# Sixteen modulation turns of the second layer placed elsewhere: six in the key and query tiles, four in the dilated attention, four in the mix, two in the up projection

## The reference, cut to what matters

```
def first_block(...):
    c_act = jax.nn.silu(c)
    for l in range(DEPTH):
        ada = (c_act @ w_ada[l] + b_ada[l])[:, None, :]
        sh1, sc1, g1, sh2, sc2, g2 = jnp.split(ada, 6, axis=-1)
        u = h * (1.0 + sc1) + sh1
        y = mixer(u, ...)
        h = layer_norm(DN_ALPHA * h + g1 * y, ...)
        u = h * (1.0 + sc2) + sh2
        y = swiglu(u, w1[l], w3[l], w2[l])
        h = layer_norm(DN_ALPHA * h + g2 * y, ...)
```

## Time and profile before

| | |
|---|---|
| median of 3 runs | 2356.89 us (2355.12 to 2361.71) |
| the profiled execution | 2354.97 us |
| its span in the trace | 2353.2 us |
| mean granted clock of PE | 0.996 |
| busy: PE / DVE / ACT / POOL | 2279.4 / 1382.9 / 503.1 / 243.5 us |

### The profile page before, as it was taken

One profiled execution on the slowest core, in us unless ns is written; L12 is line 12 of the kernel. 1 busy time (PEld: TensorE's weight loads), 2 busy tenths in 40 slices (PEclk: granted clock), 3 DMA queues, 4 the chain that ended last, 5 costly groups with the idle time before them and its releaser, 6 DMA issues.

```text
span 2353.2 us, 29622 instructions
## 1 busy us (share of the span) xinstructions
PE 2279.4 (97%) x11910; PEld 1850.9 (79%) x11910; DVE 1382.9 (59%) x2532; ACT 503.1 (21%) x1083; POOL 243.5 (10%) x165
## 2 busy tenths in 40 slices
PE   7999999999999999999999999999999999989998
PEld 5888588799768885878988655588888887667987
DVE  5764234644746433367876677675566448756455
ACT  1222220110011223201010365322200023433200
POOL 0000001331000000013310000000000001001332
PEclk9999999999999999999999999999999999999999
DMA  9863438545476343575654411433433324345442
GB/s 393 331 222 108 146 117 311 213 155 177 173 275 226 108 142 127 180 258 200 210 201 170 144 36 40 149 108 126 143 116 124 110 90 162 125 152 179 157 166 81
DMA packets 163511, 391.34 MB, mean 166 GB/s; under 512 B 6448, under 2 KB 10928, under 8 KB 160560
## 3 DMA queue, kind: packets, MB, share of 16 engines
q1 hardware_dynamic: 136736, 285.03, 34.0%
q0 software_dynamic: 24080, 93.69, 11.1%
q10 hardware_dynamic: 2560, 10.72, 1.2%
HBM read 388.37 MB, written 1.05 MB: 165 GB/s over the span
## 4 chain that ended last, share of the span: by engine, by line
PE 91%; DVE 6%; ACT 1%; issue 1%; DMA 0%; SPq 0%; DVEq 0%; ACTq 0%
PE bank L548 89%; DVE arena L2087 3%; PE bank L546 2%; DVE arena L2093 2%; ACT arena L1440 1%; DMA arena<-in_w_ada 0%; DVE arena L2090 0%; ACT arena L1443 0%; DVE junk L2093 0%; DVE arena L3039 0%; ACT L1440 0%; DVE arena L2225 0%; SPq L3201 0%; DVE arena L2156 0%; SPq L3193 0%
## 5 line engine op out<-in xcount | busy, mean ns | idle before, releaser
L548 PE MATMUL bank<-arena 128*128 128x256 f32 (+5 forms) x11422 | 2225.8, 363 | 45.8 <-DVE arena L2087 17.8
L548 PEld LDWEIGHTS bank<-arena 128*128 128x128 f32 (+2 forms) x11422 | 1794.0, 189 | 464.7 <-issue 248.8
L2087 DVE TENSOR_TENSOR arena<-arena 128x1024 f32<-128x1024 f32 (+8 forms) x535 | 446.6, 849 | 228.6 <-PE bank L548 195.6
L1440 ACT ACTIVATE arena<-arena 128x512 f32<-128x512 f32 (+5 forms) x427 | 213.6, 521 | 804.3 <-DVE arena L2087 457.9
L2093 DVE SCALAR_TENSOR_TENSOR arena<-arena 128x1028 f32<-128x1028 f32 (+6 forms) x367 | 308.9, 858 | 97.6 <-DMA arena<-in_w_ada 77.4
L2087 DVE TENSOR_TENSOR arena<-arena,bank 128x256 f32<-128x256 f32 (+2 forms) x326 | 150.1, 485 | 157.0 <-PE bank L548 147.3
L3279 POOL DMA_DIRECT2D arena<-in_w_ada x88 | 62.7, 712 | 1728.0 <-DVEq L2102 1717.4
L1443 ACT ACTIVATE arena<-bank 128x512 f32<-128x512 f32 (+1 forms) x199 | 109.0, 598 | 439.3 <-PE bank L548 414.9
L2087 DVE TENSOR_TENSOR arena<-bank,arena 128x512 f32<-128x512 f32 (+3 forms) x103 | 70.1, 690 | 206.4 <-PE bank L548 184.4
L1440 ACT ACTIVATE arena<-bank 128x256 f32<-128x256 f32 (+1 forms) x121 | 50.2, 432 | 504.9 <-PE bank L548 504.2
L2093 DVE SCALAR_TENSOR_TENSOR arena<-bank,arena 128x254 f32<-128x254 f32 (+2 forms) x184 | 78.1, 469 | 51.1 <-PE bank L546 34.1
(11 more groups left out here) (37 smaller groups left out, 221.3 us busy)
## 6 DMA issues: line engine op xcount, KB each, us to landing
arena<-in_w_ada POOLq DMA_DIRECT2D x88, 1028.0 KB, 5.6
arena<-in_w_in SPq DMA_DIRECT2D x84, 1024.0 KB, 7.2
arena<-in_w SPq DMA_DIRECT2D x56, 1024.0 KB, 5.5
arena<-in_w_mlp_in SPq DMA_DIRECT2D x32, 1024.0 KB, 7.0
arena<-in_w_mlp_out SPq DMA_DIRECT2D x32, 1024.0 KB, 7.3
arena<-in_w_gla SPq DMA_DIRECT2D x12, 1024.0 KB, 6.9
arena<-in_w_ada SPq DMA_DIRECT2D x16, 514.0 KB, 19.4
arena<-in_w_a SPq DMA_DIRECT2D x8, 1024.0 KB, 7.0
```

Of the source, the lines that this page charges most:

```text
L548: ins = nc.tensor.matmul(out, lhsT, rhs, start=start, stop=stop)
L1440: return nc.scalar.activation(out, x, f, **kw)
L2087: return V.tensor_tensor(out, x, y, op)
```

## The change

The sixteen turns n = 36 to 51 keep their order and their content and get other places: one after each of the key and query tiles n = 2, 4, 6, 8, 9, 11 (the four one-condition turns and two others), one after each of the four attention units, one after WA 0, WB 0, WB 1 and WB 2 in the mix, and one after the up panels 3 and 6. POOL's queue is changed with it: the weight sums of panels 0 to 4 stand before load 52, those of 5 to 7 before load 53, those of 8 and 9 before load 54. Layer 0 is unchanged.

```
-UP_TURNS = (1, 3, 4, 6, 7, 9)
+UP_TURNS = (3, 6)
+MINI_TURNS = (2, 4, 6, 8, 9, 11)
+FIRST_UP_JOB = 52
...
+                beside = iter([(q, [("ada", 0)]) for q in ADA_TAIL] +
+                              [(q, [("next", 0)] if l + 1 < DEPTH else [("next", 1), ("nextx", 2)]) for q in ADA_NEXT] +
+                              [(q, [("ada", 1), ("adax", 2)]) for q in ADA_LATER[:4]])
...
                 for n in range(12):
                     for h, s in minis(n):
                         dve_mini(h, s)
+                    if l == DEPTH - 1 and n in MINI_TURNS:
+                        beside_mix(1)
                 for u in range(SLOTS // 2):
...
+                    if l == DEPTH - 1:
+                        beside_mix(1)
                 for p in range(2):
...
-                        beside_mix((1, 1, 1 - l, 0)[j])
+                        beside_mix(((1, 1, 1, 0), (1, 0, 0, 0))[l][j])
...
-                        beside_mix((1, 5, 0, 3 - l)[j])
+                        beside_mix(((1, 5, 0, 3), (1, 1, 1, 0))[l][j])
...
                     if l == DEPTH - 1 and at in UP_TURNS:
-                        j = UP_TURNS.index(at)
-                        if j < 2:
-                            beside_mix(1)
-                        else:
-                            ada_turn(6 + j, [("ada", 1), ("adax", 2)])
-                        if j == len(UP_TURNS) - 1:
+                        beside_mix(1)
+                        if at == UP_TURNS[-1]:
...
-                if 48 <= n < 54:
-                    for at in range((-1, *UP_TURNS)[n - 48] + 2 if n > 48 else 0, min(UP_TURNS[n - 48] + 2, len(UP))):
+                if FIRST_UP_JOB <= n < FIRST_UP_JOB + 3:
+                    for at in ((0, 1, 2, 3, 4), (5, 6, 7), (8, 9))[n - FIRST_UP_JOB]:
                         weight_sums(1, at)
```

More of the change, by code:

```diff
@@ L2635, in _, with beside_mix @@
                 dve.wait_ge(act_done, AC.at("silu 7"))
+                beside = iter([(q, [("ada", 0)]) for q in ADA_TAIL] +
+                              [(q, [("next", 0)] if l + 1 < DEPTH else [("next", 1), ("nextx", 2)]) for q in ADA_NEXT] +
+                              [(q, [("ada", 1), ("adax", 2)]) for q in ADA_LATER[:4]])
+                def beside_mix(n):
+                    for _ in range(n):
+                        q, conds = next(beside)
+                        ada_turn(q, conds)
+                        if q == ADA_TAIL[-1]:
+                            gate("g2")
                 for n in range(12):
```

## The result

The changed kernel takes 2364.10 us, median of 20 runs (2361.71 to 2366.99); the kernel before, on the same chip, takes 2360.32 us, median of 20 (2354.95 to 2363.83). The ratio is 1.0019 with a 95% interval of 1.0012 to 1.0026, so 2.8 to 6.1 us slower. That is inside the 0.3% called "no change", on the slow side of it, and 2364.1 us lies outside the predicted range of 2352.4 to 2361 us.

What follows compares the result with a forecast made beforehand. PE bounds the kernel, busy 2279.4 of 2353.2 us. Up projection -4.63, tiles and attention 0, mix +3.32 and clock +2.1 sum to +0.8 us; on 2354.97 us, plus 1.0, that gives 2356.8 us, range 2352.4 to 2361.

Steps and rivals of the forecast that it cites:

- no change, leaning slower: Whole kernel: +0.8 us in sum; chance 0.91 of staying within 7 us, 0.06 of slower.
- The base: Whole kernel: the profiled execution's 2354.97 us, plus 1.0 us for the mean of the two lower timed runs, 2356.0 us.
- Mix: +3.32 us: Second layer's mix: the turn after WB 2 delays mix 3, so WO's wait grows from 1.51 to 4.83 us.
- rival C: Mix: POOL's sum gets in before DVE's add for mix 3, 2.7 us later, +3.5 us in all; chance 0.11.
- Up projection: -4.63 us: Second layer's up projection: waits after panels 1 and 7 go (-2.13, -2.50 us), 1.27 us after panel 3 stays.
- ceiling of 5.9 us: Second layer's up projection: PE's four waits for DVE, 5.9 us together, cap the gain at 0.25% of the time.
- PE's clock: 2.1 us: Start of WO: the 4.83 us wait makes the granted clock fall, costing 2.1 us, between 0 and 2.8.
- Tiles and attention: 0: Key and query tiles, attention: the ten turns fit DVE's gaps, tightest spare 1.5 and 1.7 us, so cost 0.
- Rival D: Key and query tiles: loads land late, turns overrun at four tiles, 7.2 us, +8.0 us in all; chance 0.04.
- E: Up projection: the removed turns did not cause the waits, which stay, +5.4 us, 2361.4 us; chance 0.02.
- Rival B: Up projection: the wait after panel 3 goes too, another -1.27 us; chance 0.10.
- Rival A: WO: the clock holds despite the 4.83 us wait, -1.3 us in all, 2354.7 us; chance 0.13.

Runs made afterwards that it cites:

- the fourth experiment: The changed kernel with the turn behind WB 2 moved behind WA 2 and POOL's sums of up panel 5 ahead of load 52: 2352.08 us, ratio 0.9968.
- the fifth experiment: The kernel before, its six up projection turns in place, with only POOL's sums of panels 3, 5, 6, 8 and 9 one load earlier: 2359.24 us, ratio 0.9991.
- the first experiment: The changed kernel with only the turn behind WB 2 moved behind WA 2: 2353.81 us, ratio 0.9975.

## Why the prediction was wrong

The sign, "no change, leaning slower", and the two mechanisms (the waits of the removed turns go; the turn behind WB 2 makes WO wait and the clock fall) were right. Three steps failed: the base that the sum was added to, the mix term of +3.32 us, which let DVE's add go ahead of POOL's sum, and, the other way, the up projection's -4.63 us. The first two are the miss.

**The base.** The sum was made against an execution of 2354.97 us with a mean granted clock of 0.996, and 1.0 us was added. This was an execution on the lucky side. Of the 35 executions of the kernel before that ran beside the first experiments, one had 0.996, and eleven had 0.991:

| mean granted clock | 0.991 | 0.992 | 0.993 | 0.994 | 0.995 | 0.996 |
|---|---|---|---|---|---|---|
| executions | 11 | 6 | 7 | 3 | 7 | 1 |
| mean time, us | 2363.6 | 2361.5 | 2359.7 | 2358.0 | 2355.8 | 2356.4 |

Of the 30 beside the last experiments six had 0.996 and ten had 0.991. About 2 us go with each 0.001. The three runs shown had a median of 2356.89 us, the twenty have 2360.32. This step is worth 2360.32 - 2356.0 = 4.3 us of the miss of 7.3, and it says nothing about the change: with 4.3 us added to both ends the same range runs to 2365.3 us and holds the 2364.1 measured.

**"Mix: +3.32 us."** The turn is worth just that, 4.83 us of wait with POOL held back. But the forecast let DVE's add go first because it would start 0.17 us before POOL's sum. The start came out as computed (0.15 us), and DVE lost all the same, 2.38 us. That was rival C, with a chance of 0.11. Its price, +2.7 us, was 0.3 too high; its condition, "should POOL be first", read from the starts of rows, was wrong. The Trainium skill (SBUF — State Buffer, section "SBUF: two separate sides") says that of the two operations the one that starts first has the shared port for its whole length, and the other waits. That they exclude each other agrees with the rows, in the mix (3.06 us in place of 0.69) and after panel 3 (4.51 in place of 2.56). That the first to start wins does not, if the starts of the rows are taken for it: DVE's is first, and DVE lost. A race with a margin of 0.2 us should have had about even odds, not 0.11.

**"Up projection: -4.63 us."** Right in place: the waits after panels 1 and 7 went, the 1.27 us after panel 3 stayed. Too small by 1.05 us. Two things were overlooked, and both stand in the view of PE's weight loads, in the row that sums up their waits for DVE in the up projection (total, times, longest), before:

```profile
PEld bank L548 <- DVE arena L2087: 6.8, 5, 2.7
```

and after:

```profile
PEld bank L550 <- DVE arena L2089: 1.4, 1, 1.4
```

There are five waits, not four, and each of the four known is about 0.16 us longer than in PE's own row. The last three of the five, before:

```profile
1138.35 12.58 PEld L548 LDWEIGHTS bank<-arena 128*128 128x128 f32 x112 [1.43 <-DVE arena L2087]
1151.20 35.81 PEld L548 LDWEIGHTS bank<-arena 128*128 128x128 f32 x320 [0.27 <-DVE arena L2087]
1189.67 10.46 PEld L548 LDWEIGHTS bank<-arena 128*128 128x128 f32 x93 [2.67 <-DVE arena L2087]
```

The fifth, 0.27 us, stands after panel 4's turn, where the forecast said "none". By these rows 6.8 - 1.4 = 5.4 us had to go, against 5.68 measured. The "ceiling of 5.9 us" of gain was too low for the same reason: the fourth experiment takes out 7.19. For the wait after panel 3 alone the two come close: 1.43 in the row of the weight load, 1.49 by the length of the stage. What PE lost beyond its weight-load rows (0.3 us in 5.7) stays unexplained.

**"PE's clock: 2.1 us."** A fall came, in place and in kind; between its bounds of 0 and 2.8 it was 1.70 us behind the wait of 4.83 and 2.61 behind 7.21. The Trainium skill (TensorE: Matmul & The Clock Gate, section "HAM oscillation — how this bites in real kernels") warned of waits between bursts, and its warning holds in these rows for the waits of 4.83, 4.84 and 7.21 us. That a fall came behind 1.99 us too, which I had not feared, is measured here alone. The prediction's evidence for a steady clock, 3.67 us of waiting with nothing lost, was luck: the same wait cost the changed kernel 6.73 - 3.81 = 2.92 us. The mean clock of the twenty runs of the changed kernel is 0.9905; that of the kernel before is 0.9929 over its 65 runs beside the experiments. 0.0025 x 2355 = 5.9 us at most. Of this the half clock that fell on a waiting PE costs nothing: in the profile, 10.2 us at half speed less 5.3 us of them with PE at work leaves 4.9 us, 2.4 us of clock. The other 3.5 us are near the loss of the medians, 3.8 us, with waits that cancel. That each of the twenty runs had this same fall is an assumption; their clocks are known, their traces are not. The 10.2 us at half speed are 0.0022 of the 0.0025; the rest, 0.7 us, is clock lost in other places.

The miss of 2364.1 - 2356.8 = 7.3 us is then: base 4.3, POOL first 2.4, up projection -1.05, clock at WO 0.5. That makes 6.15; the last 1.1 us are what is left over, and clock elsewhere (0.7 by the means) is the likely part of it.

**"Tiles and attention: 0"** held. Rival D (late loads) did not come: DVE waits for no load between 780 and 1000 us. Nor did E (the waits were not the turns'): the waits after panels 1 and 7 left with their turns. But two of the four waits were the turns' only through POOL, whose sums stood behind loads that waited for them, as the fifth experiment shows. Rival B did not come, but that third wait is POOL's, and moving one panel's sums takes it away. Rival A, the steady clock at 4.83 us of wait, came in neither of the two profiled executions with such a wait.

**The version to keep** is the change with the last turn of the mix behind WA 2 and POOL's sums of panel 5 ahead of load 52: 2352.08 us, 5.0 to 9.9 us faster than before and about 12 us faster than the change.

## What to carry to other kernels

A piece of covered work is free only where nothing that the bottleneck is waiting for stands behind it on its engine; look for the last result before each stage, and put the piece into a gap that is longer than it (here 6.24 us for 5.37), a few operations earlier. Where two engines are released by the same event and share a resource, a margin of a few tenths of a microsecond is no margin: order them by a wait or by the queue, as panel 5's sums did. And look at the mean clock of a profiled execution beside that of many runs before using its time as a base.

## What the runs showed of the hardware

**The spread of this kernel's time is PE's clock.** 2 us per 0.001 of mean clock, almost 8 us between the slowest and the fastest of its classes. The same wait is followed by a fall in one execution and by none in another. Up to the second layer's tiles the code is the same in every kernel here. The place at 651 us that is shown above, with 3.06 us of idle time and 7.10 us of matmuls before, looks like this in the first experiment:

```profile
650.21 8.80 PE L550 MATMUL bank<-arena 128*128 128x512 f32 x16 [3.06 <-issue]
```

```profile
650.00:653.00 3.00, 2.79 (x4) 1.19 (x5) 0.37 (x1) 1.51 (x5) 0.00 (x0) 0.64 0.97 410
```

The last row is its window: 0.64 of the clock, and 16 matmuls 1.70 us longer. Over the ten kernels, one profiled execution each, this wait of 3.06 us was followed by slower matmuls in seven, and so was the wait of 3.67 us at about 1920 us. Before WO wait and fall are: 1.51 us, none in six kernels; 1.99 us, 1.70 us lost; 4.83 and 4.84 us, 1.70 us lost; 7.21 us, 2.61 us lost. What decides, for a given wait, whether a fall follows in this execution stays open: no experiment here was made for it.

**A recorded start isn't a claim on the shared resource.** DVE's add of 0.69 us, started 0.15 us ahead of POOL's sum, took 3.06 us and ended after it. Whether its row starts before it has asked for the resource, or POOL has asked before its own row starts, wasn't tried.

**A wait in the up projection costs about 0.2 us more than PE's own row shows** (1.49 us by the stage's length for 1.27 in the row); the row of the weight load (1.43) shows most of that. Whether this holds for other shapes than 128x128 fp32 wasn't tried.
